# One layer of a hybrid decoder on one core: what each engine does in the last stage, where the output weights are held, and when the sample states are computed

## The reference, cut to what matters

```
proj = modulate(x) @ w_in                       # u, v and s_in
a_out = u * chunk_spatial_mix(v)
b_out, h = s5_mixer(s_in, h0)                   # y = gelu(y); y * sigmoid(y @ w_glu + b_glu)
x = x + gt1 * (concat(a_out, b_out) @ w_out)
h = modulate(rms_norm(x)); group = top1(h @ w_group); two experts = top2(h @ w_expert in the group)
moe = sum over the two experts of gate * (silu(h @ w1[e]) * (h @ w3[e])) @ w2[e]
x = x + gt2 * moe
y = rms_norm(x, g_final)                        # x * rsqrt(mean(x * x) + eps) * g_final
```

## Time and profile before

| what | value |
|---|---|
| median of three runs | 1662.95 us |
| the profiled execution | 1659.27 us |
| its span, first to last instruction | 1657.6 us |
| PE, DVE, ACT, POOL busy | 1312.3, 1015.8, 572.4, 710.7 us |
| granted TensorE clock, mean | 0.893 |
| `s5`, `mixout`, `route` with its barriers, `experts`, `final` (us from the start, rounded) | 478-628, 628-1002, 1002-1018, 1018-1518, 1518-1657 |

### The profile page before, as it was taken

The page is one execution under the profiler, slowest core; times in us unless marked ns, Lnnn a source line. Parts: engine busy times, 40 slices in busy tenths (PEclk is TensorE's granted clock), DMA queues, the critical chain, the costliest instruction groups (busy, mean ns, idle before and its releaser), DMA issues. The chain is left out here.

```text
span 1657.6 us, 25301 instructions
## 1 busy us (share of the span) xinstructions
PE 1312.3 (79%) x6323; PEld 1004.8 (61%) x6324; DVE 1015.8 (61%) x2141; ACT 572.4 (35%) x1002; POOL 710.7 (43%) x528
## 2 busy tenths in 40 slices
PE   6992899999966764999999861999999999994000
PEld 1241788888843443788888641787888887883000
DVE  7994756655617863355566454685544675761898
ACT  1122323222212123122122112685554765761332
POOL 2931322322213760344444342475432564653883
PEclk9995999999987986999999875999999999997555
DMA  8759221111137128445444416999766899984983
GB/s 230 263 159 283 74 77 51 51 61 66 45 132 93 43 79 291 153 153 186 168 178 157 140 51 233 301 382 352 271 239 245 293 382 342 343 290 185 321 301 123
DMA packets 177867, 322.74 MB, mean 195 GB/s; under 512 B 21781, under 2 KB 106069, under 8 KB 177536
## 3 DMA queue, kind: packets, MB, share of 16 engines
q1 hardware_dynamic: 162618, 276.19, 49.5%
q0 software_dynamic: 13664, 45.70, 8.0%
q10 hardware_dynamic: 1536, 0.26, 0.1%
HBM read 235.73 MB, written 86.39 MB: 194 GB/s over the span
## 5 line engine op out<-in xcount | busy, mean ns | idle before, releaser
L2081 POOL TENSOR_TENSOR down_lo<-expert_raw,down_hi (+1 forms) x64 | 155.4, 2449 | 182.6 <-ACT down_hi L2171 182.6
L2217 DVE TENSOR_TENSOR up_lo<-expert_raw,up_hi (+1 forms) x128 | 166.1, 1355 | 20.3 <-ACT up_hi L2166 20.1
L631 PE MATMUL ps_up<-up_hi,xT_hi 128*128 x400 | 161.3, 403 | 2.9 <-DVE up_lo L2217 2.9
L633 PE MATMUL ps_up<-up_hi,xT_lo 128*128 x400 | 157.3, 393 | 0.0
L632 PE MATMUL ps_up<-up_lo,xT_hi 128*128 x400 | 156.7, 392 | 0.0
L2166 ACT ACTIVATE up_hi<-expert_raw (+1 forms) x128 | 125.3, 1057 | 3.5 <-DMA expert_raw<-in_w 1.7
L631 PE MATMUL ps_out<-wout_hi,catT_hi 128*128 128x512 f32 (+1 forms) x272 | 110.9, 408 | 1.6 <-DVE catT_lo L1662 1.6
L632 PE MATMUL ps_out<-wout_lo,catT_hi 128*128 128x512 f32 (+1 forms) x272 | 109.2, 402 | 0.0
L633 PE MATMUL ps_out<-wout_hi,catT_lo 128*128 128x512 f32 (+1 forms) x272 | 109.0, 401 | 0.0
L794 POOL TENSOR_TENSOR v<-v,lng 128x512 f32<-128x512 f32 (+1 forms) x17 | 21.9, 1290 | 194.7 <-DVE v L943 194.7
L2211 DVE TENSOR_TENSOR xT_lo<-ps_xT,xT_hi 128x512 fp32r<-128x512 f32 x102 | 65.6, 685 | 54.5 <-ACT xT_hi L2159 54.4
(11 more groups left out here) (372 smaller groups left out, 3287.0 us busy)
## 6 DMA issues: line engine op xcount, KB each, us to landing
expert_raw<-in_w SPq DMA_DIRECT2D x96, 1024.0 KB, 9.4
expert_rows<-yo SPq DMA_DIRECT2D x49, 512.0 KB
wada<-in_w_ada SPq DMA_DIRECT2D x12, 2048.0 KB, 8.1
x<-in_x_prompt SPq DMA_DIRECT2D x32, 512.0 KB, 4.1
expert_rows<-blank SPq DMA_DIRECT2D x31, 512.0 KB, 4.1
x_rows<-x SPq DMA_DIRECT2D x16, 512.0 KB, 2.7
moe_in_rows<-h SPq DMA_DIRECT2D x16, 512.0 KB, 2.9
x<-x_rows SPq DMA_DIRECT2D x16, 512.0 KB, 8.4
```

Source lines behind the costliest of these rows:

```text
L631: pe.matmul(out, left(0, k), right(0, k), start=k == 0, stop=False)
L633: last = pe.matmul(out, left(1, k), right(0, k), start=False, stop=k == n - 1)
L2081: pool.tensor_tensor(down_piece(down_lo, run, m), raw_piece(run, 2, m, 1), down_piece(down_hi, run, m).bitcast(F32), ALU.subtract).then_in ...
L2217: dve.tensor_tensor(up_piece(up_lo, run, m), raw_piece(run, m // 2, m % 2, KD // 2), up_piece(up_hi, run, m).bitcast(F32), ALU.subtract).t ...
```

## The change

Three stages change.

In `s5` the four small instructions per pair go; one `tensor_copy` of 2 x 8 columns out of PSUM (`x_samp`) takes their place, `x_free` is signalled before the two sums, and eight instructions after the last pair compute all sample states.

In `mixout` the raw output weights have ten places in the buffer `expert_raw`, so no load waits for a place; the second tile's rows (`load_cat(1, 1)`) are loaded ahead of `w_out`; the router's small loads come last, with a semaphore of their own. The weights of experts 0 and 1 are loaded after tiles 14 and 15 and no longer in `route`. ACT's squares write to `mixed` (the buffer `junk3` goes), DVE chooses the last two prompt tiles' experts after the sample tile's norm, and the last scatter has its own index tiles, so that it doesn't wait for the one before. GpSimd clears the used semaphores at the stage's start.

In `final` GpSimd only gathers, up to six tiles ahead; DVE multiplies by the layer's gate as well; the root is taken for two tiles at once by `inv_sqrts`.

```diff
@@ s5, DVE, pair @@
+                    c.did(dve.tensor_copy(x_samp[:, :, ds(k, 1), :].rearrange("p i o c -> p i (o c)"), pX[:, 2 * b:2 * b + 2, 0:NSEQ]))
                     c.link(dve.tensor_tensor(rot[:, b, 3, :], R[:, NSEQ:CH], N, ALU.mult))
...
-                    c.did(dve.scalar_tensor_tensor(out=f1[:, 0, :], in0=h0r, scalar=col(S.a8_re, k), in1=R[:, 0:NSEQ],
-                                                   op0=ALU.mult, op1=ALU.add))
-                    c.link(dve.scalar_tensor_tensor(out=f1[:, 1, :], in0=h0r, scalar=col(S.a8_im, k), in1=I[:, 0:NSEQ],
-                                                    op0=ALU.mult, op1=ALU.add))
-                    dve.scalar_tensor_tensor(out=fin[:, 0, :, ds(k, 1)].rearrange("p q o -> p (q o)"), in0=h0i,
-                                             scalar=col(S.na8_im, k), in1=f1[:, 0, :], op0=ALU.mult, op1=ALU.add).then_inc(fin_ok, 1)
-                    dve.scalar_tensor_tensor(out=fin[:, 1, :, ds(k, 1)].rearrange("p q o -> p (q o)"), in0=h0i,
-                                             scalar=col(S.a8_re, k), in1=f1[:, 1, :], op0=ALU.mult, op1=ALU.add).then_inc(fin_ok, 1)
-                    dve.wait_ge(fin_ok, 2 * k + 2)
+                    dve.sem_inc(x_free, 1)
                     c.did(dve.tensor_tensor(rot[:, b, 0, :], rot[:, b, 0, :], rot[:, b, 1, :], ALU.add))
                     c.link(dve.tensor_tensor(rot[:, b, 2, :], rot[:, b, 2, :], rot[:, b, 3, :], ALU.subtract))
-                    dve.sem_inc(x_free, 1)
...
+                for n, (h, m) in enumerate(((h0r, S.a8_re), (h0i, S.na8_im), (h0r, S.a8_im), (h0i, S.a8_re))):
+                    c.did(dve.tensor_tensor(f4[:, n, :, :], h, fan(m[:, :], s8), ALU.mult))
+                c.sync()
+                for i in range(2):
+                    c.did(dve.tensor_tensor(f4[:, 2 * i, :, :], f4[:, 2 * i, :, :], f4[:, 2 * i + 1, :, :], ALU.add))
+                c.sync()
+                for i in range(2):
+                    dve.tensor_tensor(fin[:, i, :, :].rearrange("p q a -> p a q"), f4[:, 2 * i, :, :], x_samp[:, i, :, :],
+                                      ALU.add).then_inc(fin_ok, 1)
@@ mixout, SP @@
                 for n in range(NPART):
-                    if n >= RAW:
-                        sp.wait_ge(w_l, n - RAW + 1)
-                    sp.dma_start(raw_part(n), part(w_glu, w_out, n)).then_inc(w_in[n % RAW], 16)
+                    sp.dma_start(raw_part(n), part(w_glu, w_out, n)).then_inc(w_in[n], 16)
                     if n == 1:
                         sp.dma_start(bglu[:, :], a.b_glu.to_broadcast([P, DA])).then_inc(bglu_in, 16)
+                        load_cat(1, 1)
...
+                sp.wait_ge(w_l, NPART)
+                weights = expert_weights(a)
                 for i in (14, 15, 16):
                     step(i, i // 2, i % 2)
+                    if i < 16:
+                        for n in range(3):
+                            load_run(sp, S, weights, i - 14, i - 14, n)
@@ mixout, PE, end @@
+                turn_h(TP)
                 rank(7, 2)
-                turn_h(TP)
@@ mixout, GpSimd, start and end @@
+                pool.sem_clear(S.spent)
                 pool.memset(blank[:, :], 0.0).then_inc(blank_ok, 1)
...
                 scatter(7, 2)
-                scatter_end(7)
-                scatter(8, 1)
+                pool.wait_ge(slot_ok, 9)
+                for k in range(2):
+                    pool.indirect_dma_start(
@@ mixout, DVE, end @@
-                    if last:
-                        select(7, 2)
                     dve.wait_ge(sq_ok, i + 1)
...
-                ranks(7, 2)
+                select(7, 2)
                 evac_h(TP)
+                ranks(7, 2)
                 slots(7, 2)
@@ route, SP @@
-                weights = expert_weights(a)
-                for run in range(2):
-                    for n in range(3):
-                        load_run(sp, S, weights, run, run, n)
+                pass
@@ final, GpSimd @@
+                for i in range(NT):
                     r, b = rows_of(i), i % NB
+                    if i >= NB:
+                        pool.wait_ge(x_ok, i - NB + 1)
...
-                    pool.tensor_tensor(yg[0:r, b, 1, :], yg[0:r, b, 1, :], g[0:r, :], ALU.mult).then_inc(mul_ok, 1)
@@ final, DVE @@
+                for i in range(NT):
                     if i + 2 < NT:
-                        add_rows(i + 2, (i + 2) // NB, (i + 2) % NB)
-                    if i + 1 < NT:
-                        residual(i + 1, (i + 1) // NB, (i + 1) % NB)
-                    norm(i, n, b)
+                        gated(i + 2)
+                    if i + 3 < NT:
+                        add_rows(i + 3)
+                    if i + 2 < NT:
+                        residual(i + 2)
+                    if i % 2 == 1:
+                        root(i - 1, 2)
+                        norm(i - 1, 0)
+                        norm(i, 1)
```

More of the change, by code:

```diff
@@ L193, in build @@
             assert [t.num for t in used] == list(S.spent)
+            del used[:]
             s5(nc, S, a, o)
         spent.close()
+        spent, names = names, ExitStack()
+        S.spent = range(used[0].num, used[-1].num + 1)
+        assert [t.num for t in used] == list(S.spent)
+        S.raw = sb(ctx, "expert_raw", [P, 2, 3, KD * DE])
+        S.w_in = [[sem(f"w{t}_loaded{q}") for q in range(2)] for t in ("1", "3", "2")]
         S.slot_d = dram("slot_tokens", (NE * CAP, P), I32)
@@ L1321, in mixout @@
         ident = S.ident
-        mod_in, mod_s, w_in, w_h, w_l = sem("mod2_loaded"), sem("mod2_sample_loaded"), [sem(f"weights_loaded{i}") for i in range(RAW)], sem("weights_hi"), sem("weights_lo")
+        NPART = 2 + KD
+        mod_in, mod_s, w_in, w_h, w_l = sem("mod2_loaded"), sem("mod2_sample_loaded"), [sem(f"weights_loaded{i}") for i in range(NPART)], sem("weights_hi"), sem("weights_lo")
         a_in, x_in = [sem("cat_loaded0"), sem("cat_loaded1")], [sem("x2_in0"), sem("x2_in1")]
@@ L1651, in gated @@
                     dve.wait_ge(x2_ok, 2 * i)
+                    if h == 0:
+                        dve.wait_ge(sq_ok, i)
                     g = gate_s if r == NS else gate
@@ L1685, in logits @@
                     dve.wait_ge(l_mm, i + 1)
+                    if isinstance(i, int) and i == 0:
+                        dve.wait_ge(router_in, 16 * 4)
                     dve.tensor_tensor(lg[0:r, b, :], pZ[0:r, 0:NR], br[0:r, :], ALU.add).then_inc(l_ok, 1)
@@ L2311, in _ @@
             def _(pool):
-                def gather(i):
+                for i in range(NT):
                     r, b = rows_of(i), i % NB
+                    if i >= NB:
+                        pool.wait_ge(x_ok, i - NB + 1)
+                        pool.sem_inc(pool_seen, 1)
                     for k in range(2):
@@ L2357, in _, with add_rows @@
                 c = Steps(dve, ch)
-                def add_rows(i, n, b):
-                    r = rows_of(i)
+                def add_rows(i):
+                    r, b = rows_of(i), i % NB
                     dve.wait_ge(one_ok, i + 1)
@@ L2364, in add_rows, with gated @@
                                              in1=yg[0:r, b, 0, :], op0=ALU.mult, op1=ALU.add).then_inc(two_ok, 1)
-                def residual(i, n, b):
-                    r = rows_of(i)
+                def gated(i):
+                    r, b = rows_of(i), i % NB
+                    dve.wait_ge(two_ok, i + 1)
+                    if i == TP:
+                        dve.wait_ge(samp_in, 16 * NSEQ)
+                    g = gate_s if i == TP else gate
+                    dve.tensor_tensor(yg[0:r, b, 1, :], yg[0:r, b, 1, :], g[0:r, :], ALU.mult).then_inc(mul_ok, 1)
@@ L2368, in residual, with root @@
+                def residual(i):
+                    r, b = rows_of(i), i % NB
                     dve.wait_ge(mul_ok, i + 1)
-                    dve.wait_ge(x_in[b], 16 * n + 16)
+                    dve.wait_ge(x_in[b], 16 * (i // NB) + 16)
                     dve.tensor_tensor(x3[0:r, b, :], x3[0:r, b, :], yg[0:r, b, 1, :], ALU.add).then_inc(x_ok, 1)
-                def norm(i, n, b):
-                    r = rows_of(i)
-                    dve.wait_ge(sq_ok, i + 1)
-                    inv_sqrt(dve, c, rstd[0:r, :], ssq[0:r, b:b + 1], 1.0 / D, newton[0:r, 0:1], newton[0:r, 1:2])
+                def root(i, w):
+                    r, b = rows_of(i), i % NB
+                    dve.wait_ge(sq_ok, i + w)
+                    inv_sqrts(dve, c, rstd[0:r, 0:w], ssq[0:r, b:b + w], 1.0 / D, newton[0:r, 0, 0:w], newton[0:r, 1, 0:w])
@@ L2388, in _ @@
-                dve.wait_ge(mod_in, 16 * 2)
-                add_rows(0, 0, 0)
-                add_rows(1, 0, 1)
-                residual(0, 0, 0)
-                tiles(step)
+                dve.wait_ge(mod_in, 16 * 2)
+                add_rows(0)
+                gated(0)
+                add_rows(1)
+                residual(0)
+                gated(1)
+                add_rows(2)
```

(12 more changed lines are left out.)

116 lines of the change are left out of this document (55 added, 61 removed).

## The result

The changed kernel takes 1631.66 us, median of 4 runs (1629.6 to 1633.12); the kernel before, beside it, 1662.83 (1660.91 to 1663.92). The ratio is 0.982, 95% interval 0.9802 to 0.9838. Forecast were 1633, with a range of 1622 to 1646.

A forecast was written before the change was run, and what follows sets the result against it. It took TensorE to bound `experts` and DVE `final`, where DVE and GpSimd block each other. Terms summed to 29.4 us; 1659.27 - 29.4 = 1629.9, plus 3.7 for the median, was given as 1633 us, range 1622 to 1646.

The forecast's parts named there:

- The last stage: In `final`, moving the product to DVE and pairing roots gives 5.74 us per tile against 6.96, gaining 18.5 us.
- the clean 20: In `final`, DVE's last norm ends at 1634 instead of 1654.07, 20 us gained if transfers keep up.
- The state-space stage: In `s5`, collisions stay and a pair falls from 5.88 to 5.6 us; net 3.5 us gained, bounds 0 and 9.
- The output stage's start: Tile 1's `cat` loaded ahead of `w_out` removes TensorE's idle wait, but splits come later: 0.9 us gained, bounds 0 and 2.5.
- Its end: Output stage's end: earlier norm mostly offset by blocked products, last slot list about 1.2 us; 2 us gained, bounds 0 and 3.5.
- Routing and the experts' start: With expert loads out of routing, gathered rows and slot list come sooner: 4.5 us gained, bounds 2 and 7.
- The gathers' bound of 4.3 us: At the experts' start, gathers land in 4.3 us, the least seen, instead of about 7.5; first block starts 3.2 us earlier.
- The sum: Whole kernel: 18.5 + 3.5 + 0.9 + 2 + 4.5 = 29.4 us gained.
- The bound by transfers: Rival, 15%: transfers wholly bound the last stage, tile near 6.9 us, stage gains only 2 to 6 us: 1647.
- The starved gathers: Rival, 6%: DVE's back-to-back work in `final` delays gather instructions, two taking 7.1 us; no stage gain: 1651.
- the rival on the slower side: Rival, 3%: `final`'s 34 gather instructions hold DVE up, making the kernel slower; at 1.8 us each, 1665.
- The pairs without collisions: Rival, 8%: pairs in `s5` run free of collisions, gaining 1.27 us each, 19 in all: 1617.

The follow-up runs named there:

- the part alone: In the last-stage paragraph, the kernel before with only the new `final`: 1643.92 us; in the state-space paragraph, with only the `s5` change: 1655.34 us.
- staggered loads: Changed kernel with the last stage's loads of x2 tiles 1 to 5 issued one by one, each after the previous tile's gathered rows landed: 1628.32 us.
- the product kept on GpSimd: Kernel before with one root per two tiles in the last stage, the product with the gate still on GpSimd: 1661.49 us, ratio 0.9999.
- the loads put back: Changed kernel with the loads of experts 0 and 1 moved back into routing: 1636.52 us, ratio 0.9853.
- the parts alone: Kernel before with one part each: new last stage, 1643.92 us; output stage and routing, 1654.83 us; state-space stage, 1655.34 us.
- the light root: Changed kernel with one Newton step instead of three in the last stage's roots (work left out): 1622.40 us, ratio 0.9768.

## Why the prediction held, step by step

**The last stage** (18.5 predicted, 18.2 in the changed kernel, 17.9 in the part alone). The tile was put at 5.74 us and is 5.745; the root at 2.15 us for two tiles, and from 1601.30 to 1603.46 it is 2.16. The list behind the fifth `add_rows` was put at 86 us; it is 1627.58 - 1541.38 = 86.2. But two things inside were off and nearly cancelled. I had taken 1.5 us off the clean 20 for transfers that might not keep up, and they did: 363 GB/s with stores among them. In place of that, the fifth `add_rows` came at 31.1 instead of 29.4 us. The staggered loads show that this figure is set by what else is loading; I had read it off the old trace as if it were fixed.

**The state-space stage** (3.5 net predicted). From the first pair's start to the copy of `po` it was 104.79 us before, 99.11 in the changed kernel and 98.91 in the part alone: 5.7 to 5.9. The mechanism was right, collisions remain and set the pair; the size of two terms was off. The pair fell from 5.88 to 5.49 us, not to 5.6, so 15 pairs gave 5.9 instead of 4.2. And the eight instructions at the end held GpSimd's last pair up by 0.4 us (4.78 against 4.38), not 0.8, while the last pair's scans started 0.9 us sooner within it and lasted 0.55 longer (1.94 against 1.39). The Trainium skill (SBUF — State Buffer, Who interferes with whom) says that DVE with two SBUF inputs and GpSimd reading SBUF exclude each other, and that with at most one such input, outside DVE's two-port modes, they don't contend. The traces agree: the sums from `rot` and `rot` last 0.89 beside a product, those from `ps_x`, which is not in SBUF, keep 0.42 beside one. One row shows that one SBUF input can be enough: with the product kept on GpSimd, `newton<-ssq` of 2 columns, issued 0.98 us into the last product, lasted 2.31 us (1635.89 above), while in the kernel before the same step on 1 column kept 0.14 beside a product; which mode either ran in, no trace tells.

**The output stage's start** (0.9). 0.54 between the two profiled runs; over the stretches a of all six kernels without the part (26.3 to 27.5) and all eight with it (25.4 to 26.4), 1.1 us in the mean. As predicted, the later splits are what waits now.

**Its end** (2). 0.8 in the pair of runs, 1.0 over the rows of c. Both halves were overestimated: the slot list is worth 0.8 to 1.0, not 1.2, and the new order 0, not 0.8. I had written that the blocked products would take most of it back. All of it went, though the block is not the whole reason: with it gone, 0.5 us came back.

**Routing and the experts' start** (4.5). Stretch d fell by 4.64. From the first copy of `idx` to the transposes it is 3.3 us shorter and the slot list gives 1.4, and the loads put back take 4.0 of it away again. The gathers' bound of 4.3 us was the right value to take: the first one landed in 4.2.

**The sum.** 29.4 us were predicted by the terms, the two medians differ by 31.2, the two profiled executions by 26.2; 17.3, 6.4 and 5.8 us of the parts alone make 29.5. The five stretches that the terms name gained 29.8 between the two traces (18.2, 5.7, 0.5, 0.8 and 4.6). That this is so near is in part luck: 2.2 us too little for the state-space stage were made up by 1.6 too much for the output stage's two ends. The last step was also added wrongly: 1629.9 and 3.7 are 1633.6, not 1633. The 1662.83 of the kernel before is itself on the high side, as its medians in the three later sets were 1661.1 to 1661.8 (9 to 25 runs). The 3.7 us that I added for the median was scatter of one execution, and so are, as far as the runs tell, b and e, which changed by +0.7 and +2.5 us between the two profiled runs. Over all kernels of this study b lies between 314.7 and 317.7, whatever was in it. Stretch e lies between 493.1 and 496.0 in the seven kernels with the loads of experts 0 and 1 in `route`, and between 492.4 and 496.9 in the seven with their new place: means of 494.5 and 495.4. Scatter covers it; whether 0.9 us of it is the early loads' stays open.

**The rivals.** The bound by transfers fell to the light root, which moved 383 GB/s; with staggered loads it was 415. The starved gathers didn't come: 34 gather instructions lasted 0.93 to 2.05 us, median 0.99, with DVE's large work back to back, and DVE's large instructions kept their means of 1.28 and 1.22, which also ends the rival on the slower side (its last number is wrong in the prediction: 34 instructions at 1.8 us would make 1694, not 1665). The pairs without collisions were refuted by both sums, 0.89 and 0.95 us long.

## What to carry to other kernels

In this kernel a collision between DVE and GpSimd didn't go away by making the blocked instruction rarer; the next one with two SBUF operands took its place. Move or remove the other engine's work first, and price the shorter chain only then: here the parts were worth 7 and 0 us apart and 17 together. A DMA share near 1.0 is not yet a bound: take a little off the engine beside it and see whether the period follows. And where a stage begins by gathering, issue its plain loads in the order in which they are used.

## What the runs showed of the hardware

The DMA share does not tell the rate: 0.99 stood beside 351 as beside 363 GB/s in the changed kernel, 1.01 beside 383 with the light root, 1.03 beside 415 with staggered loads, and 1.04 beside 365 in the earlier trace rows. A DVE instruction on 8 or even 2 columns can be held up until GpSimd's instruction beside it ends: 2.31 us on 8 columns, 2.86 us on 2, of which 0.47 lie ahead of the product. With one SBUF input and 2 columns it was 2.31 us as well. An `add_rows` issued 0.97 us into a product, which itself had to wait about 0.9 for the residual ahead of it, lasted 3.38 us, the longest block seen here.
